# How far the weight splits run ahead of the evictions: from five to one along a small expert slot, and back along the next wide one

## The reference

```python
for layer in range(DEPTH):
    x = x + hybrid_mixer(x, mem, ...)            # three attention-like branches, gated, projected
    h = rms_norm(x, ffn_norm_g[layer])
    x = x + (swiglu(h, ff_w_gate_up[j], ff_w_down[j]) if layer % 2 == 0
             else moe_swiglu(h, moe_w_router[j], moe_w_gate_up[j], moe_w_down[j]))

def swiglu(h, w_gate_up, w_down):
    gt, up = jnp.split(h @ w_gate_up, 2, axis=-1)
    return (jax.nn.silu(gt) * up) @ w_down
# moe_swiglu: top 2 of 8 by router logits, softmax of the two as weights,
# y = sum over experts of weight * swiglu(tokens, gate_up[e], down[e])
```

## Time and profile before

| | |
|---|---|
| time, three runs | 1708.3 us median (1707.73 to 1708.51) |
| the profiled execution | 1706.9 us, of which the span is 1705.0 us |
| PE busy | 1627.2 us, 95% of the span |
| DVE busy | 1305.4 us, 77% |
| ACT busy | 1108.9 us, 65% |
| granted TensorE clock, mean | 0.982 of full |
| read from memory | 481.5 MB |

### The profile page before, as it was taken

The page is one execution under the profiler, slowest core; times in us unless marked ns, Lnnn a source line. Parts: engine busy times, 40 slices in busy tenths (PEclk is TensorE's granted clock), DMA queues, the critical chain, the costliest instruction groups (busy, mean ns, idle before and its releaser), DMA issues.

```text
span 1705.0 us, 20144 instructions
## 1 busy us (share of the span) xinstructions
PE 1627.2 (95%) x7594; PEld 1332.1 (78%) x7594; DVE 1305.4 (77%) x965; ACT 1108.9 (65%) x950; POOL 104.5 (6%) x123
## 2 busy tenths in 40 slices
PE   7999998999999999978999998899989899988998
PEld 5777886888887778867888887688877788876886
DVE  6654666555666546658989889999899998999985
ACT  5547554444555565536777778887698877887773
POOL 4111000000012110000200000000000000000000
PEclk9999999999999999998999999999999999999999
DMA  8544444656565544487999999999999999999990
GB/s 275 179 142 147 149 148 154 216 184 187 175 209 162 148 149 148 148 322 265 370 384 354 377 367 401 400 409 405 386 381 396 409 409 403 384 403 409 409 385 26
DMA packets 161335, 484.84 MB, mean 284 GB/s; under 512 B 12992, under 2 KB 15072, under 8 KB 161248
## 3 DMA queue, kind: packets, MB, share of 16 engines
q1 hardware_dynamic: 158112, 474.16, 76.2%
q0 software_dynamic: 3136, 9.48, 1.6%
HBM read 481.50 MB, written 2.10 MB: 284 GB/s over the span
## 4 chain that ended last, share of the span: by engine, by line
PE 83%; DVE 11%; issue 2%; ACT 2%; POOL 1%; DMA 0%; DVEq 0%; POOLq 0%; ACTq 0%
PE pa L1895 18%; PE pa L1897 18%; PE pa L1896 18%; PE ps L1997 5%; DVE exp_lo_a L1618 5%; PE ps L1895 4%; PE ps L1897 4%; PE ps L1896 4%; PE pa L2231 3%; PE pa L2232 3%; DVE exp_lo_b L1618 2%; PE ps L2260 1%; PE ps L2231 1%; PE ps L2232 1%; POOL hrs L697 1%
## 5 line engine op out<-in xcount | busy, mean ns | idle before, releaser
L1618 DVE TENSOR_TENSOR exp_lo_a<-exp_raw_a,exp_hi 128x2048 fp32r<-128x2048 f32 x240 | 538.3, 2287 | 35.2 <-ACT exp_hi L1104 34.9
L1104 ACT ACTIVATE exp_hi<-exp_raw_a 128x2048 fp32r<-128x2048 f32 x240 | 451.4, 1918 | 90.9 <-PE pa L1897 50.0
L1232 DVE TENSOR_TENSOR w_lo<-w_raw,w_hi 128x1024 fp32r<-128x1024 f32 (+2 forms) x229 | 277.4, 1226 | 135.8 <-ACT w_hi L830 126.9
L830 ACT ACTIVATE w_hi<-w_raw 128x1024 fp32r<-128x1024 f32 (+2 forms) x229 | 237.3, 1050 | 171.7 <-PE pa L1897 147.6
L1895 PE MATMUL pa<-w_hi,r 128*128 128x512 f32 x600 | 240.0, 400 | 0.0
L1897 PE MATMUL pa<-w_hi,r 128*128 128x512 f32 x600 | 234.0, 390 | 0.0
L1896 PE MATMUL pa<-w_lo,r 128*128 128x512 f32 x600 | 233.8, 390 | 0.0
L1618 DVE TENSOR_TENSOR exp_lo_b<-exp_raw_b,exp_hi 128x2048 fp32r<-128x2048 f32 x96 | 217.9, 2288 | 15.4 <-ACT exp_hi L1104 14.5
L1895 PE MATMUL pa<-exp_hi,xg 128*128 128x512 f32 x560 | 220.4, 394 | 3.4 <-issue 3.4
L1897 PE MATMUL pa<-exp_hi,xg 128*128 128x512 f32 x560 | 218.7, 391 | 0.0
L1104 ACT ACTIVATE exp_hi<-exp_raw_b 128x2048 fp32r<-128x2048 f32 x96 | 182.6, 1918 | 31.6 <-PE pa L1897 23.6
(11 more groups left out here) (299 smaller groups left out, 2269.4 us busy)
## 6 DMA issues: line engine op xcount, KB each, us to landing
exp_raw_a<-in_moe_w_gate_up SPq DMA_DIRECT2D x152, 1024.0 KB, 9.6
exp_raw_a<-in_moe_w_down SPq DMA_DIRECT2D x88, 1024.0 KB, 8.9
exp_raw_b<-in_moe_w_gate_up SPq DMA_DIRECT2D x72, 1024.0 KB, 8.4
w_raw<-in_w_in SPq DMA_DIRECT2D x104, 512.0 KB, 4.3
exp_raw_b<-in_moe_w_down SPq DMA_DIRECT2D x24, 1024.0 KB, 8.7
w_raw<-in_ff_w_gate_up SPq DMA_DIRECT2D x44, 512.0 KB, 4.5
w_raw<-in_ff_w_down SPq DMA_DIRECT2D x22, 512.0 KB, 3.5
w_raw<-in_w_mem_kv SPq DMA_DIRECT2D x16, 512.0 KB, 5.8
```

The lines of the kernel that those rows point to most:

```text
L830: act.activation(w_hi[:, s % SPLIT, 0:n], raw_slot(s)[:, 0:n], ACT.Copy)\
L1104: act.activation(exp_hi[:, place, :], exp_slots[j % EXP_RAW], ACT.Copy)\
L1232: dve.tensor_tensor(w_lo[:, s % SPLIT, 0:w], raw_slot(s)[:, 0:w], w_hi[:, s % SPLIT, 0:w].bitcast(F32), ALU.subtract)\
L1618: dve.tensor_tensor(exp_lo[j % EXP_RAW], exp_slots[j % EXP_RAW], exp_hi[:, place, :].bitcast(F32), ALU.subtract)\
```

## The change

`LATE = 1` gives way to a function of the slot and of `used`:

```diff
+def holds_back(few, after_few, used):
+
+    if few:
+        return 1 + used // 10
+    return max(1, 5 - used // 8) if after_few else 1
...
-            def expert_split(i, few, used):
+            def expert_split(i, few, used, late=1):
...
-                        if holder >= used - LATE:
+                        if holder >= used - late:
                             return
...
-                        expert_split(i, few, used)
+                        expert_split(i, few, used, holds_back(few, after_few, used))
...
-                    expert_split(i, few, 0)
+                    expert_split(i, few, 0, holds_back(few, after_few, 0))
...
             for i in range(1, 7, 2):
-                expert(i, False, True)
+                expert(i, False, True, after_few=i > 1)
                 expert(i + 1, True, False, i * STEPS)
             with act.Fori(7, slots) as i:
-                expert(i, False, False)
+                expert(i, False, False, after_few=True)
```

More of the change, by code:

```diff
@@ L57 @@
 EXP_SLAB = 2048
-EXP_RAW, EXP_RING, LATE = 14, 6, 1
+EXP_RAW, EXP_RING = 14, 6
 FF_BLOCKS = [(c, min(BW, D_FF - c)) for c in range(0, D_FF, BW)]
@@ L1120, in _, with expert @@
             tokens_hi(1, False)
-            def expert(i, few, next_few, folds=0):
+            def expert(i, few, next_few, folds=0, after_few=False):
                 nonlocal j
@@ L1608, in _, with expert_split @@
             j = 0
-            def expert_split(i, few, used, at_most=EXP_SLABS):
+            def expert_split(i, few, used, late=1, at_most=EXP_SLABS):
                 nonlocal j
@@ L1621, in expert_split @@
                     j += 1
-            expert_split(0, False, 0, 1)
+            expert_split(0, False, 0, at_most=1)
             link(dve.memset(slot_pos, 0.0))
```

## The result

The changed kernel takes 1714.29 us in the median (1710.3 to 1716.3, 9 runs) against 1707.89 us (1706.35 to 1709.05, 9 runs): a ratio of 1.0035, interval 1.0025 to 1.0045. It is slower by 6 us, where 1708 and no change was forecast. The profiled execution took 1714.29 us, its span 1712.5 us, against 1706.9 and 1705.0.

The account below looks back on a forecast made before the run. Small slots were taken as bound by DVE, wide ones by PE. 1706.9 - 13.4 given back + 13.2 handed back = 1706.7 us for the profiled execution, 1708 for a median; range for 8 in 10: 1699 to 1717.

Parts of the forecast that it names:

- What bounds the kernel: Wide slots are bound by PE, small slots by DVE: 92.4 us for splits alone against 76.4 on PE.
- First wait: Small slot, s = 1: `hidden(0)` moves behind split 13, so PE's wait shrinks from 4.74 to 2.5 us.
- Second wait: Small slot: `hidden(2)` moves behind split 33 instead of 36, so PE's wait of 5.63 us goes.
- Length of a small slot: Each small slot lasts 98.5 us, against 103.40, 102.50 and 102.97 before.
- The term of 13.4 us: Time given back by the three small slots together: 4.9 + 4.0 + 4.5 us.
- Hand-back: New PE waits in wide slots 3, 5 and 7: 4.4 us a slot, 13.2 us in all.
- its three places: Wide slot waits: 2.3 us at slab 1, 1.4 at slab 5, 0.7 after the first transposes.
- The rival: Slower, chance 0.19: the clock falls at the start of each wide slot, 3 x 3.4 = 10 us, 1718.
- Bounds: Limits on the wide slots' hand-back: nothing handed back (13.2 us less), or the waits doubled.
- the chance of slower: Two cases: clock falls at wide slot starts, 1718 us (0.19), and idle DVE in small slots, 1715 us (0.05).
- The page on DMA: Loads: its 358 GB/s would need 246 us a pair of slots; the prediction held to the trace's 409.
- The page on the clock: Half-clock stretches priced at half their length: some 20 us if pure loss; the prediction took most as cover.

Follow-up runs that it names:

- extra_small: As small_only, plus two unused DVE instructions of about 2.2 us at slabs 22 and 30 of each small slot; 1711.88 us.
- extra_wide: As small_only, plus two unused DVE instructions at slabs 22 and 30 of wide slots 3, 5 and 7; 1697.79 us.
- first_early: As small_dve, but in small slots `hidden(0)` stands two splits earlier, behind split 11 in place of 13; 1695.45 us.
- small_dve: As small_only, but small slots hold back in DVE's list alone, ACT's list being that of the kernel before; 1694.71 us.
- dve_only: The change's new numbers in DVE's list alone, small and wide slots; ACT's list stays with five splits ahead; 1703.92 us.
- small_only: The change in small slots only; slots 3, 5 and 7 issue five splits ahead as in the kernel before; 1696.35 us.
- chain_a: As small_only, but y_hi and output_lo of slots 3, 5 and 7 stand ahead of split 1 as in the change; 1708.71 us.
- the two halves of the change: Against the kernel before: holding back in small slots only, 1696.35 us, or in wide slots 3, 5 and 7 only, 1722.94 us.

## Why the prediction was wrong

- **What bounds the kernel**: right. extra_small and extra_wide show it directly, first_early shows that the first wait of PE ahead of an eviction is cover for splits.
- **First wait** 2.5 us: measured 2.54. **Second wait** gone: so it is.
- **Length of a small slot** 98.5 us: 98.66 where the clock held throughout (slot 2), 99.25 with one fall, 99.91 with two. The term of 13.4 us was mis-sized; it measured 11.0. What was left out are the falls of the clock behind waits of 1.8 and 2.5 us, to which the sum gave nothing. They are covered only in part: with ACT's list ahead (small_dve, dve_only) they cost nothing, with it held back 0.6 to 0.7 us each (99.39 and 99.31 against 98.65 in small_only), of which 0.5 are DVE's idle time ahead of split 18.
- **Hand-back**: the mechanism and its three places were right, the size was not; 13.2 was forecast and 17.0 measured. From one slab's start to the next the waits cost 2.4 to 2.7, 1.3 to 1.4 and 0.9 us against 2.3, 1.4 and 0.7, and the slab behind each lasts 0.1 to 0.2 longer: 5.2 a slot in place of 4.4, or 2.4 us over three slots. Part of it is the restart: behind a wait the second matmul starts 0.34 us after the first (1129.38, 1129.72), against 0.23 in a run. The fall of the clock in slot 3 is the rest.
- **The step that failed** is the sum of these two terms. Both were mis-sized: 13.4 given back measured 11.0, 13.2 handed back measured 17.0. They erred to the same side, by 2.4 and by 3.8 us, and two terms that nearly cancel left a sign that hung on their errors. About half of the 6.2 us is the clock, to which neither term gave anything: some 1.9 in the small slots (three falls) and 1.4 in slot 3. The other half is mostly the waits of the wide slots, 0.8 a slot longer than forecast. The rival had it that "all such falls in the expert stage stand behind waits of over 4 us" and kept it out of the sum, as a case of its own with 0.19, priced at 3.4 us a fall. The trace of before had, apart from one of 2.0 us at the last scatter, only long waits there and so said little of what short ones do; they bring the clock down too, in some slots. In the changed kernel it fell four times, once uncovered (1.6 us) and three times half covered (about 0.6 each).
- **Bounds.** For a hand-back the lower bound of the sum was nothing and the upper one doubled waits; the measured one lies 29% above the forecast. The time is inside the range of 1699 to 1717, the chance of slower was 0.24.
- **The page on DMA** (Trainium skill, DMA: Bandwidth & Descriptors, the table of ceilings, which gets its 358 GB/s a core by halving the rate that two cores share): no run of this kernel, which uses one core, is held to it; the windows above have 408 to 412 GB/s.
- **The page on the clock** (Trainium skill, TensorE: Matmul & The Clock Gate, Part 1, half the length of a stretch at half clock): right where PE is the bound, 1.6 us for 3.4 in chain_a; in a small slot first_early, beside small_dve, shows that the same stretch costs nothing as long as DVE is fed.
- What the prediction did not see at all is that the two halves of the change can be had apart, and that its own rows for the small slot already said that slab 0 to 4 can be split in a row and still be in time for the scatter. The halves do not add up exactly: alone they measured 11.8 us less and 14.8 more, 3.0 more together, where the change has 6.4. In the traces 1.1 us of the rest lie in slot 3 and 1.3 in slot 4, where the clock of the change falls behind the waits at slab 1 and at slab 39 and that of neither half did. How much of it is the luck of single executions no run settles.

## What to carry to other kernels

A wait of the busiest engine ahead of an eviction is worth removing only if the engine it waits for has idle time there; compare that engine's busy time over the stretch first, then put one instruction of known length into its list, which prices the stretch in a single run. How far work runs ahead should fall where the producer is the bound and stay high where the consumer is: in a stage where every idle microsecond of the consumer counts, the order at its start must have several pieces in hand before each eviction that depends on the consumer's own last step. And the list of an engine with slack (ACT here) need not follow that of the one without.

## What the hardware did unexpectedly

The granted clock fell to half for 3.4 us behind waits of 1.8, 2.1 and 2.5 us, in some slots and not in others of the same order: behind the first wait (2.54 us) in slots 4 and 6 of the changed kernel but not in 2, behind slab 1 in slots 3 and 7 of chain_a but not in 5. In the wide slots of chain_a it costs 1.6 us each time. At the start of slot 0 it stays at half for 3.4 or 6.8 us in kernels whose lists there are alike, and the slot lasts 120.5 to 120.9 or 121.3 to 122.1 us. Falls that come in one execution and not in the next may be a good part of the scatter of 6 us between the runs of one kernel: only one run each was profiled, but of the nine of the change the four with a mean granted clock of 0.988 or 0.989 have spans of 1708.4 to 1711.2 us, the five with 0.985 to 0.987 spans of 1712.3 to 1714.4.
